# Latent attention in one fused kernel: one square a half, norm weights in the rotation's tables and in the copies behind the transposes, and a new order of turns

## What is computed

```python
q = (rms_norm_2(c_q, g_cq) @ w_uq).reshape(B, S, 8, 96)
c_kv = rms_norm_2(c_kv, g_ckv)
k = concatenate([(c_kv @ w_uk) as heads of 64, k_rope broadcast to 8 heads], -1)
q = rms_norm_2(q, g_qnorm); k = rms_norm_2(k, g_knorm)     # over the 96 columns
q = [q[..., :64], apply_rope(q[..., 64:])]; k likewise
o = softmax(q k^T / sqrt(96), masked by chunks of 64) v     # then an rms norm per head
```

## Time and profile before

| | |
|---|---|
| median of 3 runs | 1577.87 us (1577.16 to 1578.76) |
| the profiled execution | 1579.24 us |
| its span | 1577.4 us |
| TensorE busy | 1473.9 us (93%) |
| VectorE busy | 1072.0 us (68%) |
| ScalarE busy | 720.6 us (46%) |
| GpSimd busy | 319.8 us (20%) |
| mean granted clock of TensorE | 0.969 |

### The profile page before, as it was taken

One profiled execution on the slowest core, in us unless ns is written; L12 is line 12 of the kernel. 1 busy time (PEld: TensorE's weight loads), 2 busy tenths in 40 slices (PEclk: granted clock), 3 DMA queues, 4 the chain that ended last, 5 costly groups with the idle time before them and its releaser, 6 DMA issues.

```text
span 1577.4 us, 24907 instructions
## 1 busy us (share of the span) xinstructions
PE 1473.9 (93%) x10282; PEld 1317.8 (84%) x10282; DVE 1072.0 (68%) x1804; ACT 720.6 (46%) x1223; POOL 319.8 (20%) x149
## 2 busy tenths in 40 slices
PE   7997999999998777989999999999999999999998
PEld 6885787998887765877999999999998888888886
DVE  5646554665458878662599988999965555555554
ACT  4555344554353541324454445444444444444443
POOL 0045100000025523056799920000000000000000
PEclk9998999999999988969999999999999999999999
DMA  7623342455553410024465554444455656666663
GB/s 275 209 92 103 115 160 91 161 185 192 187 157 116 120 53 2 1 67 133 151 203 170 174 161 148 148 148 147 146 163 161 188 188 188 188 189 189 188 188 122
DMA packets 64880, 235.25 MB, mean 149 GB/s; under 512 B 7424, under 2 KB 7680, under 8 KB 64512
## 3 DMA queue, kind: packets, MB, share of 16 engines
q1 hardware_dynamic: 63904, 231.60, 46.1%
q10 hardware_dynamic: 864, 2.07, 0.4%
HBM read 232.60 MB, written 1.05 MB: 148 GB/s over the span
## 4 chain that ended last, share of the span: by engine, by line
PE 80%; DVE 11%; POOL 4%; ACT 3%; issue 2%; DMA 1%; ACTq 0%; DVEq 0%; POOLq 0%
PE ps L129 78%; POOL spl L144 3%; ACT spl L141 1%; PE ps L138 1%; DVE junk L144 1%; DVE spl L144 1%; DVE prep L144 1%; DVE pm L144 1%; DMA raw<-in_w_in_a 1%; DVE pR L144 1%; DVE pm L153 1%; DVE hx L144 1%; DMA par<-in_par 1%; DVE be L144 0%; DVE ez L144 0%
## 5 line engine op out<-in xcount | busy, mean ns | idle before, releaser
L129 PE MATMUL ps<-xhl,spl 128*128 128x256 f32 x4944 | 609.6, 283 | 11.3 <-POOL spl L144 9.6
L129 PEld LDWEIGHTS ps<-xhl,spl 128*128 128x128 f32 x4944 | 593.9, 189 | 15.1 <-POOL spl L144 11.3
L141 ACT ACTIVATE spl<-raw 128x1024 fp32r<-128x1024 f32 (+1 forms) x435 | 454.2, 1048 | 328.9 <-PE ps L129 311.2
L144 DVE TENSOR_TENSOR spl<-raw,spl 128x1024 fp32r<-128x1024 f32 (+1 forms) x329 | 402.3, 1229 | 214.5 <-ACT spl L141 212.7
L129 PE MATMUL ps<-spl,Wr 128*128 128x512 f32 x1536 | 360.1, 396 | 3.3 <-DVE Wr L144 3.3
L129 PEld LDWEIGHTS ps<-spl,Wr 128*128 128x128 f32 x1536 | 289.3, 188 | 73.9 <-DVE Wr L144 3.6
L144 POOL TENSOR_TENSOR spl<-raw,spl 128x1024 fp32r<-128x1024 f32 (+1 forms) x106 | 274.9, 2609 | 297.6 <-ACT spl L141 297.1
L141 ACT ACTIVATE Wr<-GE 128x256 fp32r<-128x256 f32 x128 | 53.5, 419 | 184.9 <-PE ps L129 184.9
L141 ACT ACTIVATE GE<-ps 128x256 f32<-128x256 f32 (+42 forms) x176 | 57.1, 327 | 126.5 <-DVE GE L144 109.9
L144 DVE TENSOR_TENSOR Wr<-GE,Wr 128x256 fp32r<-128x256 f32 x128 | 54.4, 426 | 82.8 <-ACT Wr L141 82.8
L129 PE MATMUL ps<-spl,ahl 128*128 128x512 f32 x384 | 90.1, 396 | 0.0
(11 more groups left out here) (337 smaller groups left out, 1245.9 us busy)
## 6 DMA issues: line engine op xcount, KB each, us to landing
raw<-in_eu SPq DMA_DIRECT2D x128, 512.0 KB, 3.6
raw<-in_ev SPq DMA_DIRECT2D x128, 512.0 KB, 3.7
raw<-in_w_up SPq DMA_DIRECT2D x32, 512.0 KB, 3.6
raw<-in_w_down SPq DMA_DIRECT2D x32, 512.0 KB, 4.2
raw<-in_w_in_a SPq DMA_DIRECT2D x16, 512.0 KB, 5.6
raw<-in_w_pq SPq DMA_DIRECT2D x16, 512.0 KB, 3.5
raw<-in_w_rwkv SPq DMA_DIRECT2D x14, 512.0 KB, 3.8
raw<-in_w_in_t SPq DMA_DIRECT2D x8, 512.0 KB, 3.5
```

Source lines behind the costliest of these rows:

```text
L129: return Done(self, self.e and self.e.matmul(out, l, r, start=st, stop=sp))
L141: return Done(self, self.e and self.e.activation(out, a, f, bias=bias, scale=scale, accum_out=acc))
L144: return Done(self, self.e and self.e.tensor_tensor(out, a, b, op))
```

## The change

The sum of squares is taken with one square of 1536 columns a half on ScalarE and one sum on VectorE. The norm weights of the 32 rotated columns are multiplied into tables `tg` (cosine and sine by weight, eight small products on VectorE, once), so that the rotation runs on the values as they come from the projection, without waiting for the norm. The multiplication by the root becomes 16 copies a half with a column as scale on ScalarE, for which they wait for both root and rotation; they give `qk_n`, on which TensorE's transposes now wait. The norm weights of the 64 plain columns become the scale of the copies behind the transposes (there the columns lie on partitions; `g_qk` has two more columns of parameters, ones in the rotated rows). GpSimd keeps the root alone. VectorE's sums and rotations move to its calls 2 to 5, from 5, 6 and 11. PLAN gets other strings for steps 4 to 11: 29 calls of "m" fall in the twenty steps.

```diff
--- before.py
+++ after.py
@@ -29,7 +29,7 @@
 SPLIT = [i for i, p in enumerate(PIECES) if p[3]]
 TURN = {i: k for k, i in enumerate(SPLIT)}
 NEG = -1e30
-PLAN = ["mt", "mt", "mtm", "mt", "t", "", "t", "tmtm", "m", "mm", "m", "mmm", "mm", "mm", "m", "mm", "km", "kkmk", "kkm", "kkm"] + ["m"] * 18
+PLAN = ["mt", "mt", "mtm", "mt", "tm", "m", "tm", "tmtm", "mm", "mm", "mm", "mm", "mm", "mm", "m", "mm", "km", "kkmk", "kkm", "kkm"] + ["m"] * 18
 SIZE = {F32: 4, F32R: 4, I32: 4, U32: 4, BF16: 2}
 
 
@@ -398,6 +398,7 @@
         MT0 = QKf[:, 2048:3072].rearrange("p (h q) -> p h q", h=8)
         rt2 = junk[:, :].rearrange("p (i n d) -> p i n d", i=4, n=16)
         ld, aa, cum, t0, t1 = (prep[:, i, :, :] for i in range(5))
+        tg = rows[:, 2240:2496].rearrange("p (t i j d) -> p t i j d", t=2, i=4, j=2)
         gtok = rows[:, 0:1024].rearrange("p (t n) -> p t n", t=2)
         mu, kkc, kac, rkc = (gcols(k) for k in ("rwkv_mu", "k_k", "k_a", "r_k"))
         pRf = pR[:, :, :].rearrange("p a b -> p (a b)")
@@ -949,7 +950,7 @@
                     for j in range(2):
                         for hp in range(2):
                             b = pe.bank("q2T", (tb, j, hp))
-                            pe.wait_ge("rope2", tb)
+                            pe.wait_ge("qk_n", tb)
                             for q in range(4):
                                 last = pe.tp(b[0:96, q * 128:q * 128 + 128], QK[:, tb, j, hp * 4 + q, :])
                             last.then_inc("q2T_ps", (tb, j, hp))
@@ -1542,14 +1543,16 @@
                 for tb in range(2):
                     act.wait_ge("uq", (tb, 2))
                     act.wait_ge("kr", tb)
+                    act.act(sq_[:, tb, :, :], h16(tb), ACT.Square).then_inc("m_sq", tb)
+                    yield
+                for _ in range(3):
+                    yield
+                for tb in range(2):
+                    act.wait_ge("q_rs", tb)
+                    act.wait_ge("rope2", tb)
                     for j in range(16):
-                        x = act.act(sq_[:, tb, j, :], h16(tb)[:, j, :], ACT.Square, acc=qst[:, tb, 0, j:j + 1])
-                        if j == 15:
-                            x.then_inc("m_sq", tb)
-                        if j % 8 == 7:
-                            yield
-                yield
-                for tb in range(2):
+                        x = act.act(h16(tb)[:, j, :], h16(tb)[:, j, :], ACT.Copy, scale=qst[:, tb, 1, j:j + 1])
+                    x.then_inc("qk_n", tb)
                     yield
                     for j in range(2):
                         for hp in range(2):
@@ -1557,7 +1560,7 @@
                             for nm in ("al", "be", "ka", "bon"):
                                 act.wait_ge(nm)
                             act.act(qT2[:, j, hp * 4:hp * 4 + 4, tb * 128:tb * 128 + 128],
-                                    act.ps("q2T", (tb, j, hp))[0:96, :].rearrange("p (a b) -> p a b", a=4), ACT.Copy).then_inc("q2T", (tb, j, hp))
+                                    act.ps("q2T", (tb, j, hp))[0:96, :].rearrange("p (a b) -> p a b", a=4), ACT.Copy, scale=gcols("g_qk")[j][0:96, :]).then_inc("q2T", (tb, j, hp))
                             yield
                 for _ in range(2):
                     yield
@@ -1747,15 +1750,13 @@
 
             t_tmp = [None]
 
-            def rope(x1, x2, cos, sin, tmp, name, key):
-                n = x1.shape[1]
-                c, s = bc(cos, 1, n), bc(sin, 1, n)
+            def rope(x1, x2, c1, s2, c2, s1, tmp, name, key):
                 if t_tmp[0] is not None:
                     dve.after(t_tmp[0])
-                dve.tt(tmp[0], x1, c, ALU.mult)
-                dve.tt(tmp[1], x2, s, ALU.mult)
-                dve.tt(tmp[2], x2, c, ALU.mult)
-                dve.after(dve.tt(tmp[3], x1, s, ALU.mult).own())
+                dve.tt(tmp[0], x1, c1, ALU.mult)
+                dve.tt(tmp[1], x2, s2, ALU.mult)
+                dve.tt(tmp[2], x2, c2, ALU.mult)
+                dve.after(dve.tt(tmp[3], x1, s1, ALU.mult).own())
                 dve.tt(x1, tmp[0], tmp[1], ALU.subtract)
                 t_tmp[0] = dve.tt(x2, tmp[2], tmp[3], ALU.add).then_inc(name, key)
 
@@ -1834,7 +1835,8 @@
                 xv = qk[:, tb, :].rearrange("p (n d) -> p n d", d=64)
                 for nm in ("qk0", "qk1"):
                     dve.wait_ge(nm + ("_v", "_a")[tb])
-                rope(xv[:, :, 0:8], xv[:, :, 8:16], trig[:, 1, tb, 0:8], trig[:, 0, tb, 0:8], [rt[:, i, :, 0:8] for i in range(4)], "rope", tb)
+                c, s = (bc(trig[:, i, tb, 0:8], 1, 16) for i in (1, 0))
+                rope(xv[:, :, 0:8], xv[:, :, 8:16], c, s, c, s, [rt[:, i, :, 0:8] for i in range(4)], "rope", tb)
             for tb in range(2):
                 dve.wait_ge("mem_rs", tb)
                 dve.ts1(xn[:, tb, :], hB[:, tb, :], s_mem[tb][1], ALU.mult).then_inc("mem_n", tb)
@@ -2150,23 +2152,29 @@
                 dve.tr(Xc[:, js, :].rearrange("p a b -> p (a b)"), Yc[:, js, :].rearrange("p a b -> p (a b)")).then_inc("X0", j)
             for j in range(2):
                 w.past("w_uq", j)
+
+            for tb in range(2):
+                for i, (sc, half) in enumerate(((1, 0), (0, 1), (1, 1), (0, 0))):
+                    g = rows[:, 2048:2240].rearrange("p (j d) -> p j d", j=2)[:, :, 64 + 16 * half:80 + 16 * half]
+                    v = dve.tt(tg[:, tb, i, :, :], g, bc(trig[:, sc, tb, 8:24], 1, 2), ALU.mult).own()
+            dve.after(v)
             dve.wait_ge("w_used", AT["w_ukv"] + 1)
             for tb in range(2):
                 dve.cp(vM[:, tb, :], dve.ps("ukv", (tb, 1))[:, :]).then_inc("vM", tb)
             mix(8, 12)
 
             def mla():
-                for _ in range(4):
-                    yield
                 for tb in range(2):
+                    yield
                     dve.wait_ge("m_sq", tb)
+                    dve.after(dve.red(qst[:, tb, 0, :], sq_[:, tb, :, :], ALU.add).own())
                     dve.ts(qst[:, tb, 1, :], qst[:, tb, 0, :], 1.0 / 96, 1e-6, ALU.mult, ALU.add).then_inc("q_ms", tb)
+                    yield
+                    rope(QK[:, tb, :, :, 64:80], QK[:, tb, :, :, 80:96], *(bc(tg[:, tb, i, :, :], 2, 8) for i in range(4)),
+                         [rt2[:, i, :, :].rearrange("p (j h) d -> p j h d", j=2) for i in range(4)], "rope2", tb)
                 yield
                 for tb in range(2):
-                    dve.wait_ge("qk_n", tb)
-                    rope(h16(tb)[:, :, 64:80], h16(tb)[:, :, 80:96], trig[:, 1, tb, 8:24], trig[:, 0, tb, 8:24], [rt2[:, i, :, :] for i in range(4)], "rope2", tb)
-                    yield
-                    for _ in range(4):
+                    for _ in range(5):
                         yield
                 isq = 96 ** -0.5
                 for hp in range(2):
@@ -2572,14 +2580,6 @@
                     yield
                 for tb in range(2):
                     root("q", qst[:, tb, 1, :], tb)
-                for tb in range(2):
-                    pool.wait_ge("m_sq", tb)
-                    pool.wait_ge("ld_rows")
-                    v = [pool.tt(QK[:, tb, j, :, :], QK[:, tb, j, :, :], bc(rows[:, 2048 + 96 * j:2144 + 96 * j], 1, 8), ALU.mult).own() for j in range(2)]
-                    pool.after(v[-1])
-                    pool.wait_ge("q_rs", tb)
-                    x = h16(tb)
-                    pool.tt(x, x, bc(qst[:, tb, 1, :], 2, 96), ALU.mult).then_inc("qk_n", tb)
                 yield
                 for tb in range(2):
                     for _ in range(5):
@@ -2722,6 +2722,7 @@
           "rwkv_mu": I["rwkv_mu_2"], "w0": I["w0_2"], "a0": I["a0_2"], "k_k": I["k_k_2"], "k_a": I["k_a_2"], "r_k": I["r_k_2"],
           "g_ffn": I["g_ffn_2"], "g_final": I["g_final"]}
     pk = {k: cols(v) for k, v in pk.items()}
+    pk["g_qk"] = np.stack([np.concatenate([I[k].reshape(-1)[0:64], np.ones(64, np.float32)]) for k in ("g_qnorm_2", "g_knorm_2")], 1)
     poff, _ = offsets(pk)
     rows = np.concatenate([row(I[k]) for k in ("g_final", "ln_x_w_2", "ln_x_b_2", "g_qnorm_2", "g_knorm_2", "lambda_q1",
                                                 "lambda_k1", "lambda_q2", "lambda_k2")], 1)
```

## The result

The changed kernel takes **1589.97 us** (median of four runs, 1589.01 to 1592.32) against 1578.32 for the kernel before beside it (four runs, 1577.16 to 1579.09): ratio **1.0077**, 95% interval 1.0059 to 1.0094. So it is slower, as forecast, but by 0.77% and not by 0.36%: 6.5 us above the 1583.5 of the forecast and 0.5 above the upper end of its range. The profiled execution has 1589.01, its span is 1586.9, and TensorE's mean granted clock fell from 0.969 to 0.961.

What follows compares the result with a forecast made beforehand. The latent-attention stage, four instruction streams in PLAN's fixed order, was taken as the bound. Terms -4.8 + 28.5 - 18.0 = +5.7 us took the profiled 1579.24 to 1584.9, less 1.4 to the median: 1583.5, range 1575.5 to 1589.5.

Steps and rivals of the forecast that it cites:

- Squares, sums, tables, GpSimd's work: Latent attention: square about 1.5 us, sum 1.75, tables nothing; 12.8 us of GpSimd and 5.8 of VectorE's first rotation saved.
- Copies: 16 scaling copies on ScalarE before each half's transposes: about 0.27 us each, 4.4 a half, behind the `ktok` copy.
- the walk: Lining up the four engine streams under the new PLAN, each piece at today's duration, 0.07 us from release to start.
- rival "no change": Copies take only the lower bound, 2.8 us a half: +2.0 us, 1579.9; chance 0.20.
- First part: Up to VectorE's first subtraction of the third level: 617.1, today 615.09; the first transpose's 8 us gain is given back.
- Second part: From there to the last subtraction: VectorE works 28.3 us without a gap, to 645.4; `MV` starts 2.0 us later.
- rival "slower still": Roots hold the rotations (1585.3), and half clock behind two new stalls adds 4 us: 1589; chance 0.14.
- Third part: `MV` to transposition of `ya`: TensorE 22.7 us without a gap; `ya` at 670.9, 4.8 us earlier than today.
- From `ya` to the last output product: Transposition of `ya` to end of `out_u(1)`: 28.5 us, today 18.0, as all three state steps queue behind it.
- rival "faster": State products find room in TensorE's waits for `ya`, so only the earlier `ya` remains: -4.8 us, 1573.1; chance 0.16.
- Tail: Behind the last output product nothing changes: no transfer added, first weight splits and loads 4 us earlier, nothing waiting for them.
- The rule against the change: GpSimd's root contends with VectorE's rotation for shared SBUF interfaces: counted as nothing; in full 1.8 us more, 1585.3.

Runs made afterwards that it cites:

- run with fillers: The changed kernel with 47 transposes of the identity, which nothing reads, in TensorE's waits: 1582.12 us, ratio 1.0037.
- kernel with 25 calls: The changed kernel with its own first eight PLAN strings and thinner ones behind, 25 attention calls in the twenty steps, not 29: 1583.74 us, ratio 1.0037.
- kernel with the old head and 29 calls: The changed kernel with the first eleven PLAN strings of the kernel before and fuller ones behind, 29 attention calls in the twenty steps: 1591.72 us, ratio 1.0075.
- third order: The changed kernel with another PLAN, searched for the new arithmetic, 24 attention calls in the twenty steps, copies early: 1568.70 us, ratio 0.9932.

## Why the prediction was right or wrong

By its own steps, each as the traces have it:

- **Squares, sums, tables, GpSimd's work: right.** 1.53 a square (1.5), 1.75 a sum (1.75), both products by GpSimd gone, and the rotation at 2.2.
- **Copies: right.** 4.36 and 4.37 a half (4.4), behind the `ktok` copy as said; those of half 0 end 0.6 us behind the walk's time (597.51 against 597.9 - 0.95), those of half 1 2.2 us behind it (610.67 against 609.4 - 0.95). The rival "no change" by cheap copies fell with their price. The sentence that free copies leave the walk's end where it is today was right within 2.4 us.
- **First part: 3.9 us short.** The third level's first subtraction is at 620.04 (lines below); the forecast was 617.1, less the 0.95 of the earlier start 616.1. The products at 589.60, 593.88 and those behind the two stalls were priced at the 1.15 of full clock and took 1.97, and the transposes beside them 1.1 for 0.66. This is the step that failed: durations of today's rows were carried into places behind new waits, where the clock is not that of today. The run with fillers shows it by removing it for this part and the next together: `MV` comes 69.3 us behind the stage's start, not 76.2.
- **Second part: 3.9 us short, the same step.** 32.2 us (620.04 to 652.24) instead of 28.3. VectorE was not saturated any more: TensorE at half clock from 633 to 647 let it wait 1.21, 0.42 and 1.82. The rival "slower still" named the right mechanism, half clock behind the new stalls, but had only five products of the first part in it and a chance of 0.14; the second stretch no case had. That its 1589 is near the 1590.0 measured is therefore partly luck: its other source, the roots, cost nothing, and the errors of the second part and the third nearly cancel.
- **Third part: 3.6 us long.** From `MV` to `ya` 23.2 us (651.08 to 674.27), forecast 26.8. I took `MV` and the products behind it at half clock, as before they are in part (`MV` 4.76 for 32 in the earlier trace rows is between the two prices, about 3.8 and 7.3); in the new order they run at full (`MV` 1.97 and 1.90 for 16 each, `TAT` 1.09 each where it is 1.98 and 1.91). The same error with the other sign, and the two traces with and without fillers agree on it (646.61 to 669.79 is 23.2 too).
- **From `ya` to the last output product: right.** 28.7 us, forecast 28.5. That the three state steps would queue behind `ya` was the forecast's core, and the kernel with 25 calls brings the 18.1 back. With it falls the rival "faster".
- **Tail, taken as unchanged: 1.5 us short.** From the first product by `w_o` to the last group 27.5 us (702.74 to 730.22) for 26.0; one group behind a 3.17 us wait takes 8.44, where before it takes 7.18 behind 2.75.

VectorE's first subtraction of the third level and the last of the fifth, in the change:

```profile
620.04 1.39 DVE L144 TENSOR_TENSOR pm<-pm,ps 64x512 f32<-64x512 f32 x2
...
650.85 1.39 DVE L144 TENSOR_TENSOR pm<-pm,ps 64x512 f32<-64x512 f32 x2
```

The terms make 5.7 + 3.9 + 3.9 - 3.6 + 0.2 + 1.5 = 11.6; by the traces the stage is 11.7 longer (155.3 us from its start to the start of the last group by `w_o`, 143.6 before). The two profiled executions differ by 9.8 only (1589.01 and 1579.24): the stage starts 0.95 earlier, and the rest is gained behind it, which no run here explains. So the direction and the mechanism (the order gives all back and the state steps queue) stood, and the size was off by the clock. The kernel with fillers, in which most of the first two is gone, comes out at +5.8. That this meets the forecast's +5.7 is partly luck: in its trace the stage is only 3.1 us longer than before (146.7 for 143.6) and the third part's 3.6 us are still in it.

**The rule against the change.** The trace has GpSimd's root of half 0 from 582.63 to 585.54 and the rotation's four products from 584.02 at 1.43, as in the earlier trace rows without any GpSimd work. The second root and the second rotation lie beside each other too:

```profile
588.19 2.90 POOL L144 TENSOR_TENSOR qst<-qst,neghalf 128x16 f32<-128x16 f32 x1 [2.66 <-DVE qst L147]
590.22 1.39 DVE L144 TENSOR_TENSOR junk<-QK,rows 128x256 f32<-128x256 f32 x4
```

A root of 16 columns holds VectorE up by nothing that the trace can show, so counting nothing for it was right. The Trainium skill (SBUF — State Buffer, Who interferes with whom) calls the port pair that GpSimd and VectorE share an exclusive lock, so by it the rotation should have waited for the root, and these rows do not agree. The 7.19 of the earlier trace rows beside 3.59 us multiplications agree with it in kind.

## What to carry to other kernels

Take the duration of a TensorE piece from a row at the clock of its new place, not of its old one: behind a new wait like those of 3.44 and 4.28 us here write the half-clock price, and take it away where such a wait goes. For waits of about 2 us the rows here go both ways: behind the 2.02 us before 631.39 in the change the next inversion product is at full clock (1.15) and the one after it at half (1.97 at 633.03), behind the 2.11 us before 642.69 in the kernel with the old head and 29 calls the next products stay at full clock (1.15 and 1.14). Where streams of work are interleaved by a fixed table, a cheaper operation is worth only what the table lets through, so change the arithmetic, then search the table again, and test both against the old arithmetic in its own best table. An operation "on the path" is so by its place: taking 15 of 16 copies out gave 9.8 us in one order and nothing in another.

## What was not expected of the hardware

- 47 idle transposes of about 0.14 us each, 6.5 us of TensorE in its waits, made the whole 6.4 us faster. In the third order 40 of them in a wait of 6.18 us gave TensorE 2.13 us and made the stage no shorter, since the next wait grew by as much.
- TensorE can be busy without a gap and stay at half clock. In the kernel after, behind the wait for `ya`, it is so until the products by `w_o`:

```profile
682.00:688.00 6.00, 6.00 (x57) 5.88 (x59) 1.15 (x4) 0.00 (x0) 1.63 (x2) 0.50 0.42 147
688.00:694.00 6.00, 6.00 (x51) 5.76 (x50) 1.71 (x4) 0.00 (x0) 0.00 (x0) 0.50 0.01 3
694.00:700.00 6.00, 6.00 (x48) 5.88 (x47) 4.05 (x9) 0.66 (x2) 1.63 (x2) 0.50 0.00 0
```

These are products of 64 columns; in the third order, without the long wait ahead of them, the same products run at full clock (2.00 for 16, above). What sets the one or the other, beyond the wait ahead of it, no run here settles.
